# One decoder layer on one core: the sample group's B and C rows sent through DRAM, and three edits around the output projections

## The chip, the cores and the metric

The kernel runs on one core of a Trainium2 chip (trn2). The metric is the device time of one execution in microseconds (us). The median of three runs stands for a kernel.

## The reference, cut to what matters

One layer of a hybrid decoder works on 512 prompt tokens and 8 sample tokens (each with its own past) with the same weights, in float32. A combined projection gives queries and latents for multi-head latent attention (16 heads), and z, x, B, C and dt for a state-space branch (32 heads in 8 groups, state size 128). The part that the change touches first is the state-space step of the 8 sample tokens. For every group, head channel `p`, sample `b` and state index `n`:

```python
state_new[b, p, n] = exp(dt*a) * state[b, p, n] + (dt*x)[b, p] * B[b, n]
y[b, p]            = sum_n C[b, n] * state_new[b, p, n] + d_skip * x[b, p]
...
o_ssm  = rmsnorm_per_group(y * silu(z))
o_attn = attention(...)                                  # for samples: softmax over 2048 paged keys
merged = sigmoid(gate_a) * (o_attn @ w_br_attn) + sigmoid(gate_b) * (o_ssm @ w_br_ssm)
x      = x + rmsnorm(merged @ w_out)
x      = x + rmsnorm(w_down @ relu(w_up @ rmsnorm(x))**2)
```

B and C lie with `n` on the partitions, while the states have `p` on the partitions. So the 128 numbers of B for each sample are needed as a row, the same on all 128 partitions.

## The kernel before, in words

Everything is laid out with channels on the partitions and the T = 520 tokens along the free axis. Each float32 product is made of three passes of TensorE: rounded weight times rounded input, rounded weight times the rest of the input, rest of the weight times rounded input. Weights stream in chunks of 512 KB, in one fixed order, through two slots: SP loads a chunk into `w_stage`, ACT rounds it into `w_hi` (`round_chunk`, L939), POOL subtracts to get `w_lo` (`split_chunk`, L469, four pieces). `linear` (L521) multiplies one chunk of 8 tiles: 48 matmuls of 260 columns, 32 with `w_hi` and then 16 with `w_lo`. Its result goes to one of two slots of the PSUM tensor `lin`; the slots alternate in the order of the lists `..._LIN`, and `free_slot` waits until DVE has released the result before the last (semaphore `lin_free`, counted in DVE's order).

The program's stages are: a start (latents, scan sums), group 0 to 8, eight rows of sample attention, the two output projections, and the MLP (multi-layer perceptron).

*Groups.* Group i projects the inputs of state-space group i (x0, x1, b, c, z0, z1, queries, keys) and, between these projections, does the rest of group g = i - 1: prompt attention (two heads in 8 blocks u), the scan in four pieces c, and the 8 products s0 to s7 with `w_br_ssm`, added to `acc` by DVE (L1729). The last group (i = 8) has gate projections ga0 to ga6 in place of new inputs. For each c, PE issues `scan_front(c)`, `scores(2c+1)`, `project(c+1)` with `transposes(2c)` inside, `values(2c)`, `transposes(2c+1)` (L676), `scan_back(c)`, `scores(2c+2)`, `values(2c+1)`. DVE follows with `normalise` (L1589), `row_max`, `scan_front`, `raw_samples` (L1461, which frees the slot of x0, x1 and so on), `scan_back` (L1616).

*The samples' state in group g.* PE spreads B over the partitions with 8 matmuls of a broadcast column against the identity (`on_all("bB", 2)`, L728), behind s7 and ahead of the first scores and `project(0)`. Each matmul shows as two in the profile. DVE multiplies it from PSUM with dtx (L1643, L1644), adds it to the scaled states (L1647), and then runs `raw_samples(0)`. Behind `project(1)` PE spreads C in the same way (`on_all("bC", 3)`); `sample_y(t)` on DVE multiplies it with the states (L1659) and sums (L1662), for t = 0 in front of `scan_back(0)` and for t = 1 behind `row_max(2)`. The slot of bC is released in `sample_y(1)` (L1661).

*ACT at the end of a group* has `round_chunk(SB)`, the last tanh, 16 scalings of the states (L1044), `round_chunk` of the next group's x0, and at the start of the next group the load of the convolution's history (`history`, L994), `round_chunk` of x1, and then the copies of `project(0)` out of PSUM (L1017, L1018).

*Rows.* Row b scores one sample against its 2048 keys (L796, L804, L809), then PE runs the merge of row b - 1 (`row_merge`, L843 to L847), a gate projection (gb0 to gb7, with two small products inside) and `row_values(b)` (L835). Row 4 has two projections, ga7 and gb4. In SP's queue each row has 4 page loads of keys for row b + 2 (L398), the next weight chunks (L365), and 16 page loads of latent rows; ACT's queue has the other 12 loads of keys (L983).

*Behind row 7* there are: the last merge, `row_out` and the split of the latents on DVE and ACT, then 48 small matmuls of 16 columns with the value weights (L876, here called OV), two copies (L1264, L1809), the branch projection (8 tiles E0 to E7; DVE merges each with the gates, L1819 to L1824) and the output projection (8 tiles F0 to F7). E0 waits for `ov_ready`; F0 waits until all eight merged tiles are there (`mg_ready`).

## Time and profile before

| | |
|---|---|
| median of 3 runs | 1499.13 us (1494.08 to 1499.55) |
| the profiled execution's own time | 1498.6 us |
| its span, first to last instruction | 1496.8 us |
| mean granted TensorE clock | 0.965 |
| PE busy | 1403.4 us, 94% |
| DVE, POOL, ACT busy | 58%, 41%, 38% |
| PE line L521 in the chain that ended last | 52% of the span |
| page loads in the rows stage | DMA engines busy 0.8 to 1.0 of the time |

The span is what the sums below are made in; 1.8 us of the execution's own time lie around it. "Busy" of PE counts overlapping matmuls, so the time of a stretch is read from the start of one instruction to the start of another. The granted clock 1.00 is 2.4 GHz, 0.50 is 1.2 GHz.

### The profile page before, as it was taken

How to read it: one execution, taken by the hardware profiler on the slowest of the kernel's cores; microseconds unless marked ns; L12 is line 12 of the kernel's file. 1: busy time of each engine (PE TensorE's matmuls, PEld its weight loads, DVE VectorE, ACT ScalarE, POOL GpSimd, SP SyncE). 2: the span in 40 equal slices, each digit the busy share in tenths (PEclk: the TensorE clock that was granted, in tenths of full speed). 3: DMA queues.
4: the chain of work that ended last, by engine and by line, in shares of the span. 5: the costliest groups of instructions: out<-in, count | busy, mean ns of one | idle time of the engine just before them, and what ended most of it. 6: DMA issues, size and time to landing. Idle time of an engine off the chain costs nothing.

```text
span 1496.8 us, 28722 instructions
## 1 busy us (share of the span) xinstructions
PE 1403.4 (94%) x11570; PEld 1306.8 (87%) x11570; DVE 860.8 (58%) x1713; ACT 567.9 (38%) x1162; POOL 608.0 (41%) x753
## 2 busy tenths in 40 slices
PE   4999999999999999999999999899579999999994
PEld 4998898988989889898989777799569999999994
DVE  6487878878788787878875443233442222222226
ACT  3344544544444444454544212222233222323221
POOL 4452352443525343352523222344344445444541
PEclk9999999999999999999999999799779999999997
DMA  4223222323233233222245899242113233323231
GB/s 159 85 80 90 80 90 72 103 75 91 75 98 93 71 91 101 77 87 90 74 124 158 264 339 337 77 142 86 42 43 98 87 98 89 97 89 94 87 99 58
DMA packets 109589, 160.47 MB, mean 107 GB/s; under 512 B 16497, under 2 KB 83569, under 8 KB 109457
## 3 DMA queue, kind: packets, MB, share of 16 engines
q1 hardware_dynamic: 54864, 127.32, 27.1%
q10 hardware_dynamic: 54592, 31.33, 7.2%
q8 instruction: 91, 1.49, 0.4%
q14 instruction: 42, 0.34, 0.1%
HBM read 145.87 MB, written 12.74 MB: 106 GB/s over the span
## 4 chain that ended last, share of the span: by engine, by line
PE 66%; DVE 15%; SPq 4%; ACT 4%; issue 2%; DMA 1%; POOL 1%; DVEq 0%; POOLq 0%; ACTq 0%
PE lin L521 52%; SPq L398 3%; PE lin L728 2%; PE Pb L683 1%; PE Pb L554 1%; PE lin L624 1%; DVE arena L1496 1%; DVE arena L1659 1%; DVE ysum L1662 1%; ACT arena L1144 1%; PE Pb L667 1%; DVE sm L1581 1%; PE Pb L676 1%; DMA w_stage<-in_wall 1%; DVE arena L1589 1%
## 5 line engine op out<-in xcount | busy, mean ns | idle before, releaser
L469 POOL TENSOR_TENSOR w_lo<-w_stage,w_hi 128x256 fp32r<-128x256 f32 x736 | 587.2, 829 | 831.1 <-ACT w_hi L939 831.1
L521 PE MATMUL lin<-act_hi,w_hi 128*128 128x260 f32 x1760 | 369.3, 292 | 16.7 <-DVEq L1661 4.3
L521 PE MATMUL lin<-act_lo,w_hi 128*128 128x260 f32 x1760 | 359.2, 286 | 0.0
L521 PEld LDWEIGHTS lin<-act_hi,w_hi 128*128 128x128 f32 x1760 | 276.2, 193 | 32.2 <-issue 21.3
L521 PEld LDWEIGHTS lin<-act_lo,w_hi 128*128 128x128 f32 x1760 | 277.3, 193 | 0.0
L939 ACT ACTIVATE w_hi<-w_stage 128x1024 fp32r<-128x1024 f32 x184 | 193.5, 1052 | 204.5 <-PE lin L521 152.8
L521 PE MATMUL lin<-act_hi,w_lo 128*128 128x260 f32 x1760 | 235.6, 287 | 0.0
L521 PEld LDWEIGHTS lin<-act_hi,w_lo 128*128 128x128 f32 x1760 | 221.7, 191 | 0.4 <-issue 0.4
L521 PE MATMUL lin<-mid_hi,w_hi 128*128 128x260 f32 x1024 | 210.3, 287 | 2.0 <-issue 2.0
L521 PE MATMUL lin<-mid_lo,w_hi 128*128 128x260 f32 x1024 | 207.4, 284 | 0.0
L521 PEld LDWEIGHTS lin<-mid_hi,w_hi 128*128 128x128 f32 x1024 | 160.5, 191 | 3.6 <-issue 3.2
L521 PEld LDWEIGHTS lin<-mid_lo,w_hi 128*128 128x128 f32 x1024 | 159.5, 191 | 0.0
L521 PE MATMUL lin<-mid_hi,w_lo 128*128 128x260 f32 x1024 | 148.8, 282 | 0.0
L521 PEld LDWEIGHTS lin<-mid_hi,w_lo 128*128 128x128 f32 x1024 | 133.7, 188 | 0.0
L1876 DVE TENSOR_TENSOR acc<-acc,lin 128x520 f32<-128x520 f32 x64 | 44.6, 696 | 121.4 <-PE lin L521 120.5
L1855 DVE TENSOR_TENSOR arena<-lin,arena 128x520 f32<-128x520 f32 x32 | 22.4, 699 | 128.9 <-ACT arena L1288 128.9
L1496 DVE SCALAR_TENSOR_TENSOR arena<-arena,small 128x544 f32<-128x544 f32 x64 | 67.4, 1053 | 2.0
L1111 ACT ACTIVATE arena<-Pb,sm 128x128 f32<-128x128 f32 (+1 forms) x64 | 33.8, 528 | 90.8 <-DVE sm L1582 90.8
L1729 DVE TENSOR_TENSOR acc<-acc,lin 128x520 f32<-128x520 f32 x64 | 44.4, 693 | 26.5 <-PE lin L521 25.7
L554 PE MATMUL Pb<-ones,arena 128*65 128x1 f32 x400 | 29.1, 207 | 31.7 <-POOL arena L490 15.5
L554 PEld LDWEIGHTS Pb<-ones,arena 128*65 128x65 f32 x400 | 28.5, 156 | 33.7 <-POOL arena L490 16.3
L1288 ACT ACTIVATE arena<-lin 128x520 f32<-128x520 f32 x32 | 19.4, 606 | 99.6 <-PE lin L521 99.6
(259 smaller groups left out, 1868.3 us busy)
## 6 DMA issues: line engine op xcount, KB each, us to landing
w_stage<-in_wall SPq DMA_DIRECT2D x184, 512.0 KB, 3.6
arena<-in_cache ACTq DMA_DIRECT2D x80, 144.0 KB, 4.3
arena<-in_state ACTq DMA_DIRECT2D x16, 512.0 KB, 5.5
out_stateT<-arena ACTq DMA_DIRECT2D x16, 512.0 KB, 4.1
o_attn<-in_cache SPq DMA_DIRECT2D x64, 128.0 KB, 3.8
arena<-in_cache SPq DMA_DIRECT2D x64, 128.0 KB, 4.2
arena<-in_cache SPq DMA_DIRECT2D x48, 144.0 KB, 3.9
arena<-in_xT SPq DMA_DIRECT2D x8, 520.0 KB, 5.4
```

The lines of the kernel that those rows point to most:

```text
L398: sp.dma_start(dst(j), d["cache"][bass.ds(page, 1), :, lo:hi].rearrange("a p c -> p (a c)")).then_inc(landed, 16)
L469: low = pool.tensor_tensor(w_lo[:, slot, part], w_stage[:, slot, part], w_hi[:, slot, part].bitcast(F32), ALU.subtract)
L521: mm = pe.matmul(lin[:, pl.slot, hf, 0:HALF], w[:, ch.slot, off:off + P], r[:, hf * HALF:(hf + 1) * HALF], start=(k == 0 and p == 0), stop ...
L554: mm = pe.matmul(out[:, c:c + 1], src[:, k, TOKT * c:TOKT * (c + 1)], ones[:, 0:1], start=(k == 0), stop=(k == n - 1))
L728: mm = pe.matmul(lin[:, pl.slot, b // 4, (b % 4) * P:(b % 4 + 1) * P], xc[:, k, SAMP0 + 4 * b:SAMP0 + 4 * b + 1].to_broadcast([P, P]), ide ...
L939: act.activation(w_hi[:, ch.slot, :], w_stage[:, ch.slot, :], ACT.Copy).then_inc(S["w_hi_done"], 1)
L1111: act.activation(Pq[:, pb, 0:(q + 1) * P], Pb[:, pb, 0:(q + 1) * P], ACT.Exp, bias=sm[:, 2 + pb:3 + pb], scale=SM_SCALE, accum_out=sm[:, 4 ...
L1288: act.activation(cols(relu[:, j % 2, :]), lin_cols(pl), ACT.Relu).then_inc(S["relu_a"], 1)
L1496: link(dve.scalar_tensor_tensor(a, raw[:, k, t:t + CONVW], tap(t), a, ALU.mult, ALU.add))
L1729: dve.tensor_tensor(cols(acc[:, m, :]), cols(acc[:, m, :]), lin_cols(pl), ALU.add).then_inc(S["lin_free"], 1)
L1855: dve.tensor_tensor(cols(relu[:, j % 2, :]), lin_cols(pl), cols(relu[:, j % 2, :]), ALU.mult).then_inc(S["lin_free"], 1)
L1876: dve.tensor_tensor(cols(acc[:, m, :]), cols(acc[:, m, :]), lin_cols(pl), ALU.add).then_inc(S["lin_free"], 1)
```

## The change

1. *B and C through DRAM.* DVE copies the 8 sample columns of B and of C into a small tile `smp` (`samples_apart`). ACT stores each 4 KB to a DRAM tensor (`samples_out`), waits for it, and loads it back to all 128 partitions, 512 KB each (`samples_in`), into `B_all` and `C_all`. The 16 spreading matmuls are gone and with them their two places in `lin`. DVE now reads B and C from SBUF, with a stride of 8 elements, and makes and adds the product of one half after the other (`sample_states`). In the first group with a scan (g = 0), `sample_states` moves from ahead of `normalise(0)` to behind `raw_samples(1)`.
2. *A gate moved.* ga7 goes from row 4 to behind the last row's merge, in front of OV.
3. *OV and E0.* OV does the passes of a half with `w_hi` before it waits for `w_lo`. E0 is done by halves of the tokens: the first half (260 prompt tokens) no longer waits for the samples' values.
4. *Output projection singly.* F0 waits for each merged tile at its turn; the E and F loops are written out.

```diff
-STEADY_LIN = (["bB", "x0", "sA0", "x1", "bC", "sA1", "b", "sA2", "c", "sA3", "z0", "z1", "uq0", "uq1", "uk", "uv", "ql"]
+STEADY_LIN = (["x0", "sA0", "x1", "sA1", "b", "sA2", "c", "sA3", "z0", "z1", "uq0", "uq1", "uk", "uv", "ql"]
...
-ROW_GATES = [["gb0"], ["gb1"], ["gb2"], ["gb3"], ["ga7", "gb4"], ["gb5"], ["gb6"], ["gb7"]]
+ROW_GATES = [["gb0"], ["gb1"], ["gb2"], ["gb3"], ["gb4"], ["gb5"], ["gb6"], ["gb7"]]
...
@@ PE, group @@
-                on_all("bB", 2)
                 if g:
                     first_scores()
                     project(0)
+                pe.wait_ge(S["xc_ready"], g * 4 + 4)
...
                     project(c + 1, between=lambda: transposes(u))
-                    if c == 0:
-                        on_all("bC", 3)
...
@@ PE, behind the rows @@
             row_merge(NB - 1)
+            linear(fixed(LIN_LAST), fixed(CH_LAST), K8, act_rhs())
...
+            for half in range(2):
+                ch = fixed(CH_OV + half)
+                pe.wait_ge(S["w_hi_done"], ch.index + 1)
+                for pr in range(4 * half, 4 * half + 4):
+                    for k in range(2):
+                        values_of(pr, k, ((w_hi, olat_hi), (w_hi, olat_lo)), ch)
+                pe.wait_ge(S["w_split"], ch.index + 1)
+                for pr in range(4 * half, 4 * half + 4):
+                    for k in range(2):
+                        mm = values_of(pr, k, ((w_lo, olat_hi),), ch)
...
             pe.wait_ge(S["oa_ready"], KT)
-            pe.wait_ge(S["ov_ready"], 2)
...
-            pe.wait_ge(S["mg_ready"], KT)
...
+            by_halves(fixed(LIN_E), fixed(CH_E), mid_rhs(0, KT), (S["ov_ready"], 2))
+            for m in range(1, KT):
+                linear(fixed(LIN_E + m), fixed(CH_E + m), K8, mid_rhs(0, KT))
+            for m in range(KT):
+                linear(fixed(LIN_F + m), fixed(CH_F + m), K8, act_rhs(), rhs_ready=None if m else (S["mg_ready"], 0))
...
@@ ACT, group @@
+                def samples_out(t):
+                    act.wait_ge(S["smp_ready"], i * 2 + t + 1)
+                    act.dma_start(o["samples"][i, t], smp[:, t, :]).then_inc(S[f"smp_out{t}"], 16)
+
+                def samples_in(t):
+                    act.wait_ge(S[f"smp_out{t}"], i * 16 + 16)
+                    if t == 0:
+                        act.wait_ge(S["st_new"], i * 2)
+                    else:
+                        act.wait_ge(S["xc_ready"], i * 4 + 4)
+                    act.dma_start((B_all, C_all(i))[t], o["samples"][i, t].rearrange("n b -> (n b)").partition_broadcast(P)
+                                  ).then_inc(S[("b_in", "c_in")[t]], 16)
...
                     scaled_state(0)
                     scaled_state(1)
+                    samples_out(0)
                 round_chunk(c_chunk(i, "SB").next())
+                if has_in:
+                    samples_in(0)
+                    samples_out(1)
+                    samples_in(1)
...
@@ DVE, group @@
+                def samples_apart(t):
+                    dve.wait_ge(S[f"smp_out{t}"], i * 16)
+                    dve.wait_ge(S["xc_ready"], i * 4 + (3 + t if has_rest else 4))
+                    dve.tensor_copy(smp[:, t, :], xc[:, 2 + t, SAMP0:CONVW:4]).then_inc(S["smp_ready"], 1)
...
-                link(dve.tensor_tensor(sT[:, 0], bB, spread(dtx[:, 0, :], STATE), ALU.mult))
-                dve.tensor_tensor(sT[:, 1], bB, spread(dtx[:, 1, :], STATE), ALU.mult).then_inc(S["lin_free"], 1)
...
+                def sample_states():
+                    dve.wait_ge(S["xc_ready"], g * 4 + 4)
+                    dve.wait_ge(S["st_scaled"], g * 2 + 2)
+                    link(dve.tensor_tensor(dtx[:, :, :], sdec_all[:, g, :, 0:8], xc[:, 0:2, SAMP0:CONVW:4], ALU.mult))
+                    dve.wait_ge(S["b_in"], g * 16 + 16)
+                    for t in range(2):
+                        new = sT if g else sT_first
+                        link(dve.tensor_tensor(new, B_all.rearrange("p (n b) -> p b n", b=NB), spread(dtx[:, t, :], STATE),
+                                               ALU.mult))
+                        dve.tensor_tensor(sS[:, t], sS[:, t], new, ALU.add).then_inc(S["st_new"], 1)
+                        dve.wait_ge(S["st_new"], g * 2 + (t + 1))
...
                 def sample_y(t):
+                    dve.wait_ge(S["c_in"], g * 16 + 16)
+                    link(dve.tensor_tensor(sC[:, :, :], C_all(g).rearrange("p (n b) -> p b n", b=NB), sS[:, t], ALU.mult))
...
                     if c == 0:
+                        if g == 0:
+                            sample_states()
                         sample_y(0)
```

In group 0, ACT has `samples_out` and `samples_in` for both t at its end, behind the last tanh and ahead of group 1's `history`. Behind the rows, ACT evacuates ga7 between `round_chunk(CH_OV + 1)` and `round_chunk(CH_E)`.

## Rows read from the trace of the kernel before

**Rows 1.** One group by windows: stretch, PE, PEld, DVE, ACT, POOL, PEclk, DMA share, GB/s.

```profile
477.00:566.00 89.00, 87.28 (x707) 79.45 (x707) 73.28 (x144) 43.55 (x108) 36.76 (x40) 1.00 0.30 88
```

**Rows 2.** PE's waits from 209 to 744 us: total, times, longest.

```profile
PE lin L521 <- DVEq L1661: 3.2, 6, 0.5
```

**Rows 3.** Timeline of PE from 391 to 423 us (start, us).

```profile
392.30 1.95 PE L728 MATMUL lin<-ident,arena 128*128 128x128 f32 x16
...
407.70 1.95 PE L728 MATMUL lin<-ident,arena 128*128 128x128 f32 x16
...
409.94 0.44 PE L676 MATMUL Pb<-ident,arena 128*128 128x128 f32 x2
...
422.50 0.65 PE L676 MATMUL Pb<-ident,arena 128*128 128x128 f32 x4
```

**Rows 4.** The chain that ended last, where `project(1)` starts.

```profile
401.96 3.88 PE lin L521 x32
```

**Rows 5.** Timeline of DVE over the same stretch.

```profile
394.35 1.22 DVE L1643 TENSOR_TENSOR arena<-lin,dtx 128x1024 f32<-128x1024 f32 x1 [0.68 <-PE lin L728]
...
396.87 3.27 DVE L1647 TENSOR_TENSOR arena<-arena 128x1024 f32<-128x1024 f32 x2
401.17 0.17 DVE L1461 COPY arena<-lin 128x8 f32<-128x8 f32 x1 [1.03 <-ACT arena L1018]
...
408.66 0.17 DVE L1461 COPY arena<-lin 128x8 f32<-128x8 f32 x1 [1.50 <-ACT arena L1018]
...
412.41 0.60 DVE L1616 SCALAR_TENSOR_TENSOR arena<-arena,small,Pb 128x128 f32<-128x128 f32 x2
...
421.82 0.49 DVE L1589 TENSOR_SCALAR arena<-arena,sm 128x512 f32<-128x512 f32 x1
```

**Rows 6.** Timeline of ACT at the end of the group.

```profile
389.22 1.05 ACT L939 ACTIVATE w_hi<-w_stage 128x1024 fp32r<-128x1024 f32 x1
```

**Rows 7.** DMA issues: count, KB each, median us from issue to landing.

```profile
w_stage<-in_wall SPq DMA_DIRECT2D x184, 512.0 KB, 3.6
...
arena<-in_state ACTq DMA_DIRECT2D x16, 512.0 KB, 5.5
...
arena<-in_hist ACTq DMA_DIRECT2D x8, 64.0 KB, 2.3
```

**Rows 8.** Two lines of DVE by source: ns min/median/max.

```profile
L1647 DVE TENSOR_TENSOR arena<-arena x16: 1224/1590/1642, 132.3 to 753.3; 128x1024 f32<-128x1024 f32 x16
...
L1643 DVE TENSOR_TENSOR arena<-lin,dtx x8: 1223/1224/1224, 129.8 to 749.5; 128x1024 f32<-128x1024 f32 x8
```

**Rows 9.** Timeline of DVE at the start of group 1.

```profile
128.88 0.17 DVE L1461 COPY arena<-lin 128x8 f32<-128x8 f32 x1 [2.13 <-DMA arena<-in_hist]
```

**Rows 10.** Timeline of PE: the first product of rows 4, 5 and 6.

```profile
886.20 0.28 PE L796 MATMUL lin<-qlb,snb 128*1 128x32 f32 x4
...
911.08 0.28 PE L796 MATMUL lin<-qlb,snb 128*1 128x32 f32 x4
...
924.58 0.28 PE L796 MATMUL lin<-qlb,snb 128*1 128x32 f32 x4
```

**Rows 11.** Waits from 840 to 960 us.

```profile
PE lin L521 <- ACT w_hi L939: 1.6, 1, 1.6
```

**Rows 12.** Timeline of PE behind row 7, and at F0.

```profile
956.19 0.35 PE L876 MATMUL lin<-olat_hi,w_hi 128*128 128x16 f32 x1 [2.35 <-issue]
...
967.43 0.77 PE L521 MATMUL lin<-mid_hi,w_hi 128*128 128x260 f32 x2 [0.86 <-issue]
...
1018.27 0.51 PE L521 MATMUL lin<-act_hi,w_hi 128*128 128x260 f32 x2 [2.92 <-DVE act_lo L1824]
```

**Rows 13.** Windows (columns as in rows 1) of three stretches.

```profile
954.00:971.00 17.00, 13.95 (x64) 13.92 (x65) 1.91 (x9) 4.02 (x6) 7.34 (x11) 0.50 0.27 88
189.00:192.00 3.00, 3.00 (x17) 3.00 (x16) 2.62 (x12) 1.24 (x2) 0.80 (x2) 0.56 0.36 115
1019.00:1022.00 3.00, 3.00 (x16) 3.00 (x16) 2.97 (x1) 0.81 (x1) 2.11 (x4) 0.50 0.00 0
```

More of the change, by code:

```diff
@@ L235, in build_layer @@
         sm = sb("sm", [P, 8])
+        smp = sb("smp", [P, 2, NB])
         sms = sb("sms", [P, 8])
@@ L880, in _, with values_of @@
-            mm.then_inc(S["lin_done"], 1)
-            pe.wait_ge(S["oa_ready"], KT)
-            pe.wait_ge(S["ov_ready"], 2)
-            for i in range(0, KT // 2):
-                for j in range(2):
-                    linear(looped(LIN_E, 2, i, j), looped(CH_E, 2, i, j), K8, mid_rhs(0, KT))
-            pe.wait_ge(S["mg_ready"], KT)
-            for i in range(0, KT // 2):
-                for j in range(2):
-                    linear(looped(LIN_F, 2, i, j), looped(CH_F, 2, i, j), K8, act_rhs())
+            def values_of(pr, k, passes, ch):
+                off = (pr % 4) * 256 + k * P
+                for w, x in passes:
+                    r = x[:, k * P:(k + 1) * P].rearrange("p (b h) -> p b h", b=NB)[:, :, 2 * pr:2 * pr + 2]
+                    mm = pe.matmul(lin[:, pl.slot, 0, 16 * pr:16 * pr + 16], w[:, ch.slot, off:off + P], r,
+                                   start=(pr == 0 and k == 0 and w is w_hi and x is olat_hi),
+                                   stop=(pr == 7 and k == 1 and w is w_lo))
+                    if pr % 4 == 0 and k == 0 and w is w_hi and x is olat_hi:
+                        open_chunk(ch, mm)
+                return mm
@@ new lines, in _, with by_halves @@
+            mm.then_inc(S["lin_done"], 1)
+            def by_halves(pl, ch, rhs, second_ready):
+                pe.wait_ge(S["w_hi_done"], ch.index + 1)
+                free_slot(pl)
+                for hf in range(2):
+                    if hf:
+                        pe.wait_ge(second_ready[0], second_ready[1])
+                    part = slice(hf * HALF, (hf + 1) * HALF)
+                    for k in range(KT):
+                        for n in range(2):
+                            mm = pe.matmul(lin[:, pl.slot, hf, 0:HALF], w_hi[:, ch.slot, K8[k]:K8[k] + P], rhs[k][n][:, part],
+                                           start=(k == 0 and n == 0), stop=False)
+                            if hf == 0 and k == 0 and n == 0:
+                                open_chunk(ch, mm)
+                    if hf == 0:
+                        pe.wait_ge(S["w_split"], ch.index + 1)
+                    for k in range(KT):
+                        mm = pe.matmul(lin[:, pl.slot, hf, 0:HALF], w_lo[:, ch.slot, K8[k]:K8[k] + P], rhs[k][0][:, part],
+                                       start=False, stop=(k == KT - 1))
+                mm.then_inc(S["lin_done"], 1)
@@ L1105, in group @@
                     act.wait_ge(S["rows_ready"], 1)
+                    for t in range(2):
+                        samples_out(t)
+                    for t in range(2):
+                        samples_in(t)
                     return
@@ L1674, in group @@
                     if c == 0:
+                        if g == 0:
+                            sample_states()
                         sample_y(0)
@@ L2062, in build @@
     o = {n: nc.dram_tensor("out_" + n, tuple(shape), F32, kind="ExternalOutput").ap() for n, shape in OUTS.items()}
+    o["samples"] = nc.dram_tensor("samples", (GROUPS, 2, P, NB), F32, kind="Internal").ap()
     build_layer(nc, d, o)
```

72 lines of the change are left out of this document (25 added, 47 removed).

## The prediction, on record before the changed kernel ran

> **What bounds the kernel now.** First the windows of one group [rows 1]: of 89.0 us PE is busy 87.28, DVE 73.28, ACT 43.55, and the DMA engines are at 0.30. The reader is to see that PE sets the pace over the whole stage, and that DVE has only some 16 us to spare. Then PE's waits [rows 2]: the one that the change touches by name, for the slot of the spread C, comes six times in six groups and costs 0.5 each. So a group is nearly one long row of matmuls, and what is taken from PE is won, unless another engine cannot follow. Whether it can is read from the timelines of PE, DVE and ACT where the work is taken out [rows 3 to 6]. Behind the groups I read the rows stage [rows 10, 11] and the places around the projections where PE stands still or runs at 1.2 GHz [rows 12, 13].
>
> A note on size first: a measurement of this kernel tells some 0.5% (7.5 us) from no change. The sums are made against the profiled execution's span of 1496.8 us, whose own time is 1498.6, 0.5 below the median of 1499.13.
>
> **B in a steady group.** PE's block for B starts at 392.30 and that for C at 407.70; the latter ends where the next work starts, and transposes(1) follow at 409.94 [rows 3]. A block of 16 instructions starts every 0.12 us, so it costs 1.95; both in eight groups are 31 us of PE's time. That is the most that this part can give, with 0.5 a group for the wait on the slot. Not all of it comes back, because DVE has a chain beside it.
>
> Before, DVE starts the first product at 394.35, when PE has spread B, adds from 396.87 to 400.13, waits for the end of project(0), and frees x0's slot at 401.34 [rows 5]. project(1), which needs that slot, starts at 401.96 [rows 4]. Without B's block PE would be there at 400.0. When is DVE there? ACT begins to round x0's chunk at 389.22, behind the scalings of the states [rows 6]. The store of B now goes out at that place. Its 4 KB are not in the trace; the smallest load there, 64 KB, lands in 2.3 us [rows 7], which gives 391.5. The broadcast load is then issued; it carries 512 KB as a weight chunk does, and that lands in 3.6, the state loads of the same size in 5.5 [rows 7]. I take 3.6, since ACT has just these one or two transfers in flight there and each partition gets one run of 4 KB as in a weight chunk: B is there at 395.1 (397.0 by the other row). DVE then has four operations of 1024 elements. The products from PSUM took 1.22 each, always; the sums with both inputs in SBUF took 1.59 in the median and 1.22 at best, beside POOL's splitting [rows 8]. Now all four read two SBUF tensors. One is over before POOL can start on x1's chunk, which ACT rounds behind these transfers; so 1.22 + 3 x 1.6 + 0.2 of semaphores = 6.2, and x0 is free at 395.1 + 6.2 + 0.2 = 401.5. project(1) starts at 401.5 in place of 401.96. Of B's 1.95 us only 0.45 are left; bounds are 1.95 (B in time, nothing collides) and a loss of 1.4 (5.5 for the landing).
>
> The Trainium skill ("SBUF — State Buffer", section "Who interferes with whom") says that a DVE instruction with two SBUF inputs contends with a GpSimd instruction that reads SBUF, and one with at most one SBUF input does not; rows 8 agree, with 1224 ns at most for one and 1642 for the other. By the rule all four could be slow, which would make 6.6 of the 6.2 and take the rest of the gain.
>
> **C in a steady group.** Before, project(1) ends at 407.70; DVE copies x1's samples at 408.66, and reaches scan_back(0) at 412.41, 4.7 behind the projection [rows 3, 5], because sample_y(0) waited for C's block. Now C has landed long before (its load is issued about 3 us behind B's). The path is 0.96 for the copy, 0.17, then 1.22 to 1.6 for the product, 1.22 and 0.23 for the rest: 3.8 to 4.2. So 0.5 to 0.9 is won on DVE, I take 0.5. From there to normalise(3), which ends at 422.31 [rows 5], DVE hardly stands still, and PE's transposes(3) at 422.50 follow on it [rows 3]: PE loses what it is early. So C's 1.95 us and the 0.53 wait behind it turn into a wait for DVE at transposes(3), all but 0.5. The two copies into smp (0.17 each, as the copy of 8 columns in rows 5) lie in the s phase, where DVE waits for PE.
>
> Sum for a steady group: 0.45 + 0.5 = 0.95 us earlier. It holds for groups 2 to 8 (gates in place of x in the last, same order): 7 x 0.95 = 6.7. Bounds a group: 3.0 (PE at 400.0, 1.95, and 1.0 for C and its wait) and -0.8 (late landing).
>
> **The first group with a scan.** ACT issues the history's load behind both round trips now. In the trace DVE waited 2.13 us for that load already [rows 9]. The store and the return wait hold it back by about 3.4 us (2.3 of landing and two issues), so x0's samples come at 132.3. That alone is covered, for sample_states (5.0) no longer stands ahead of normalise(0). But sample_states now stands ahead of sample_y(0) and scan_back(0), on DVE's full path of the last paragraph. Both together: 3.5 us later than before (between 1 and 5).
>
> **ga7's move.** Row 4 takes 911.08 - 886.20 = 24.9 us, row 5 takes 13.5 [rows 10]. Without ga7 row 4 loses 48 matmuls of 0.12 = 5.8 and the wait of 1.6 for the second chunk [rows 11]: 7.5. The chunks of the later rows have the same place in SP's queue, behind the same page loads; SP issues row 6's and row 7's chunk while PE is a row away. So 7.5 is taken; nothing if the page loads pace the rows.
>
> **Behind row 7.** Before, the last merge ends at 953.84, PE stands for 2.35, OV runs from 956.19 and E0 from 967.43, OV at 1.2 GHz throughout and E0's first 3.6 us too (0.50 up to 971) [rows 12, 13]. By that E0 takes 5.8 + 1.8 = 7.6, to 975.0: 21.1 from the merge. Now: ga7 5.8 with row_out hidden behind it, OV at 2.4 GHz 5.3 (half of 10.4), E0 5.8, whose first half covers the two copies: 16.9. But the clock fell even beside a busy PE, to 0.56 for 189 to 192, behind 32 matmuls of one column at 186 [rows 13], and OV's 48 with 16 columns did not raise it in 11 us. I take it that OV loses the clock halfway (2.7 us, with E0's start): 19.6, 1.5 us less than before. Bounds: 4.2 and 0.
>
> **F0.** PE waits 2.92 for the last merged tile and then runs 3.2 us at 1.2 GHz (the window shows three of them) [rows 12, 13]. The first seven tiles' 28 matmuls with w_hi take 3.4, more than the 2.9 that tile 7 needs. The wait is gone, and the clock's fall with it (1.6): 4.5. Its chunk was split by then already. Bounds 2.9 and 4.5.
>
> **Sum.** -6.7 + 3.5 - 7.5 - 1.5 - 4.5 = -16.7: 1498.6 - 16.7 = 1482.
>
> **The rivals.** *PE gets it all back* (B in time, DVE's chain shorter than I read it): 7 x 3.0 in place of 6.7, 1467 to 1468. For it: DVE has 16 us to spare in a group. Against it: none of them lies between 401 and 422. *The rows are paced by their loads:* page loads need bandwidth and SP's time, and ga7 only covered them: 7.5 less, 1489. For it speaks that the DMA engines are full up to row 6; against it that row 5 takes no more than PE's own 13.5. *B lands like the states,* in 5.5: 0.8 lost a group, 7 x 1.75 more than the forecast: 1494, no change. *The other side:* 128 partitions read the same 4 KB of DRAM, and no row shows such a load. PE waits for it in project(1). Each us beyond 3.6 costs 7 in all; from a landing of 7.1 us the kernel is slower by over 0.5% (1506), at 10 us it is at 1527. No kind of transfer of this size has a median above 5.5 [rows 7]. *The change doesn't do what it says* can't be for B and C; for E0's half it may be, if w_lo is what it waits for, which is in the bounds.
>
> **How the numbers follow.** The forecast (1482, own range 1475 to 1489) has 0.50, all gained back 0.20, rows paced by loads 0.12, landing of 5.5 0.11, slow broadcast 0.07. Range: 1466 (the first rival) to 1495 (the third). Faster by over 0.5% (below 1491.6): 0.49 + 0.20 + 0.09 + 0.02 = 0.80; slower 0.07; the rest 0.13.
>
> **What would show it.** DVE's first product in a group should start about 2.8 us behind the end of s7 and release project(1); PE should wait at project(1) for x0's slot (1.5) and at transposes(3) for normalise, some 3 us a group in all. A group's period should be near 88 us in place of 89. In the first group PE should wait over 3 us. Row 4 should take about 17 us. PE should not stand still between the last merge and E0, the clock fall within OV, and F0 start right behind E7. The prediction is wrong if DVE's waits for b_in are missing or over 4 us, or if rows 5 to 7 grow beyond 13.5.

## The result, and the profile after

| | before | after |
|---|---|---|
| median | 1499.29 us (4 runs) | 1514.39 us (4 runs, 1513.10 to 1517.46) |
| ratio to before, 95% interval | | 1.0112 [1.0085, 1.0139] |
| span of the profiled execution | 1496.8 us | 1511.3 us |
| mean granted clock | 0.965 | 0.960 |

The change makes the kernel slower by 15 us; I had forecast 1482. Of all executions below, two of the kernel e11 took 1719.88 and 7485.51 us, where its other four took 1487.82 to 1493.64, and are left out of its figures. To find the place, I cut the span at one instruction that every group has once: the first matmul of its statistics on PE. "Group" is here the stretch from one such start to the next.

| us | before | after | difference | forecast |
|---|---|---|---|---|
| up to the first statistics | 186.1 | 196.1 | +10.0 | +3.5 |
| six groups behind it, each | 89.06 | 91.64 | +2.58 (15.5 in all) | -0.95 (-5.7) |
| the last group | 88.8 | 93.5 | +4.7 | -0.95 |
| from there to the end | 687.5 | 671.8 | -15.7 | -13.5 |

The tail did about what was said of it, as a sum. The whole miss, 33 us, lies in the part with B and C.

The six groups are not alike. Two of them run at a granted clock of 1.00 throughout and take 90.1 and 90.2 us; the other four have stretches at the lower clock and take 91.0 to 93.4. In the kernel before, the three groups at 1.00 take 88.7 each. So at full clock a group costs 1.4 to 1.5 more, and the rest of the +2.58 is a matter of the clock. Two of the groups, columns as in [rows 1]:

```profile
377.32:470.67 93.35, 86.54 (x671) 78.60 (x671) 77.67 (x145) 42.83 (x107) 39.71 (x40) 0.96 0.31 94
470.67:560.78 90.11, 83.78 (x671) 75.63 (x671) 77.40 (x145) 42.84 (x107) 40.16 (x40) 1.00 0.34 98
```

First PE in the groups: the windows of one group's length and of the whole stretch, and PE's waits over that stretch (total, times, longest), to be held against [rows 1, 2].

```profile
477.00:566.00 89.00, 82.76 (x655) 74.82 (x656) 76.36 (x142) 41.54 (x105) 39.53 (x40) 0.99 0.33 95
209.00:744.00 535.00, 497.60 (x3905) 450.13 (x3905) 451.69 (x836) 248.69 (x622) 232.22 (x232) 0.98 0.33 95
```

```profile
PE Pb L686 <- DVE arena L1647: 17.1, 18, 1.7
PE lin L531 <- DVE arena L1510: 11.6, 6, 2.4
PE Pb L693 <- ACT arena L1165: 6.5, 6, 1.1
```

PE now stands still for DVE at the two places that the prediction named, x0's slot (L1510) and transposes (L1647), and for longer than was forecast. The third wait, for ACT (L1165), is new too. Why DVE is late is read in the timeline of one group, DVE first. It is the longest of the six (93.35). The end of s7 is at 405.1.

```profile
405.92 0.52 DVE L1699 TENSOR_TENSOR dtx<-sdec_all,arena 128x16 f32<-128x16 f32 x1
407.55 2.21 DVE L1703 TENSOR_TENSOR arena<-sga_mid,dtx 128x1024 f32<-128x1024 f32 x1 [1.11 <-DMA sga_mid<-samples]
409.80 1.23 DVE L1705 TENSOR_TENSOR arena<-arena 128x1024 f32<-128x1024 f32 x1
411.06 2.37 DVE L1703 TENSOR_TENSOR arena<-sga_mid,dtx 128x1024 f32<-128x1024 f32 x1
413.46 1.59 DVE L1705 TENSOR_TENSOR arena<-arena 128x1024 f32<-128x1024 f32 x1
415.09 0.17 DVE L1510 COPY arena<-lin 128x8 f32<-128x8 f32 x1
...
423.90 2.45 DVE L1715 TENSOR_TENSOR arena<-arena 128x1024 f32<-128x1024 f32 x1
...
429.42 2.23 DVE L1715 TENSOR_TENSOR arena<-arena 128x1024 f32<-128x1024 f32 x1
```

The transfer is in time: DVE waits 1.11 us for it and starts 2.45 behind the end of s7. But the two products with B (L1703) take 2.21 and 2.37 and the two with C (L1715) 2.45 and 2.23, where they took 1.22 before (B's in [rows 8], C's in the first line here). The lines by source (ns min/median/max), the first of the kernel before and the others of the changed one, show that no product escaped:

```profile
L1659 DVE TENSOR_TENSOR arena<-lin,arena x16: 1214/1220/1225, 141.5 to 769.8; 128x1024 f32<-128x1024 f32 x16
...
L1703 DVE TENSOR_TENSOR arena<-sga_mid,dtx x14: 2111/2244/2430, 225.4 to 778.8; 128x1024 f32<-128x1024 f32 x14
...
L1715 DVE TENSOR_TENSOR arena<-arena x16: 1984/2226/2512, 149.5 to 799.2; 128x1024 f32<-128x1024 f32 x16
```

PE's side of the same group, against [rows 3, 4]:

```profile
415.41 0.48 PE L531 MATMUL lin<-act_hi,w_hi 128*128 128x260 f32 x2 [2.42 <-DVE arena L1510]
...
422.95 0.43 PE L693 MATMUL Pb<-arena 128*64 128x128 f32 x2
...
433.84 0.52 PE L686 MATMUL Pb<-ident,arena 128*128 128x128 f32 x3 [1.66 <-DVE arena L1647]
...
437.37 0.87 PE L693 MATMUL Pb<-arena 128*64 128x128 f32 x6 [1.10 <-ACT arena L1165]
438.64 0.66 PE L686 MATMUL Pb<-ident,arena 128*128 128x128 f32 x4 [0.41 <-DVE arena L1647]
```

project(1) starts 10.3 behind the end of s7, in place of 9.5 (the timeline of PE before has its first matmul at 401.80), and then lasts 7.5 us (415.41 to 422.95) where it took 5.9 before: behind the wait of 2.42 the granted clock falls to the lower level, 0.62 on average from 416 to 420. So here a late DVE is paid twice. That is so in two of the six groups (waits of 2.42 and 2.38); in the other four the wait at project(1) is 1.51 to 1.85 and the clock stays at 1.00 behind it. transposes(3) come 33.5 behind s7, in place of 30.2. The wait for ACT at 437.37 has the same origin: ACT copies the transposed weights only behind the exponentials of the scan (435.67 to 436.94), and these follow DVE's scan_front, which starts at 434.40. It costs 1.1 in every group, and the kernel before doesn't have it.

The DMA issues, against [rows 7], show one cost more. The 4 KB store and both broadcast loads land as expected or nearly; the history's load, which now stands behind a broadcast load in ACT's queue, takes 4.7 in place of 2.3.

```profile
sga_mid<-samples ACTq DMA_DIRECT2D x8, 512.0 KB, 3.6
arena<-samples ACTq DMA_DIRECT2D x8, 512.0 KB, 4.9
arena<-in_hist ACTq DMA_DIRECT2D x8, 64.0 KB, 4.7
...
samples<-smp ACTq DMA_DIRECT2D x16, 4.0 KB, 2.2
```

In the first group with a scan nothing hides these, against [rows 9]. DVE waits 6.80 for the history, so PE waits 6.13; then PE waits 8.87 more for transposes, while DVE does the states and y of the samples (142.3 to 158.1).

```profile
132.32 0.17 DVE L1510 COPY arena<-lin 128x8 f32<-128x8 f32 x1 [6.80 <-DMA arena<-in_hist]
```

```profile
132.63 0.77 PE L531 MATMUL lin<-act_hi,w_hi 128*128 128x260 f32 x2 [6.13 <-DVE arena L1510]
158.74 0.88 PE L686 MATMUL Pb<-ident,arena 128*128 128x128 f32 x3 [8.87 <-DVE arena L1647]
```

The tail: rows 4, 5 and 6 start as follows (against [rows 10]: row 4 takes 14.2 in place of 24.9), and behind row 7 PE goes from the merge (970.98) into ga7 (972.28), OV (979.62), E0 (986.14 and, for its second half, up to E1 at 993.87) and, last line, F0 (against [rows 12]).

```profile
914.58 0.28 PE L793 MATMUL lin<-qlb,snb 128*1 128x32 f32 x4
...
928.80 0.28 PE L793 MATMUL lin<-qlb,snb 128*1 128x32 f32 x4
942.40 0.28 PE L793 MATMUL lin<-qlb,snb 128*1 128x32 f32 x4
...
970.98 0.37 PE L840 MATMUL Pb<-arena,ones 128*128 128x16 f32 x2 [0.64 <-DVE arena L1837]
...
972.28 0.48 PE L531 MATMUL lin<-act_hi,w_hi 128*128 128x260 f32 x2
...
979.62 0.18 PE L871 MATMUL lin<-olat_hi,w_hi 128*128 128x16 f32 x1
...
983.58 0.36 PE L871 MATMUL lin<-olat_hi,w_hi 128*128 128x16 f32 x1
...
986.14 0.57 PE L899 MATMUL lin<-mid_hi,w_hi 128*128 128x260 f32 x1
...
993.87 0.41 PE L531 MATMUL lin<-mid_hi,w_hi 128*128 128x260 f32 x2
...
1034.19 0.40 PE L531 MATMUL lin<-act_hi,w_hi 128*128 128x260 f32 x2
```

PE stands nowhere between the merge and F0 (1034.19). OV runs its small matmuls every 0.11 us up to 983.58 and every 0.21 from there: the clock falls within OV, after 4.0 of its 6.5 us, and is back when E0's second half starts (990.99). F0 starts right behind E7.

### The profile page after: what moved, and what is told of

Its sections match the earlier page's. It is cut to its first block and busy times, and to the rows that moved or that the text cites. A ratio compares the mean times of both kernels' runs of the same rounds, so it can differ in the third digit from the quotient of the medians.

```text
span 1511.3 us, 28274 instructions
## 1 busy us (share of the span) xinstructions
PE 1381.0 (91%) x11314; PEld 1284.0 (85%) x11314; DVE 894.8 (59%) x1729; ACT 565.5 (37%) x1162; POOL 627.5 (42%) x753
## 5 line engine op out<-in xcount | busy, mean ns | idle before, releaser
L479 POOL TENSOR_TENSOR w_lo<-w_stage,w_hi 128x256 fp32r<-128x256 f32 x736 | 606.7, 855 | 825.9 <-ACT w_hi L963 825.9
L531 PE MATMUL lin<-act_hi,w_lo 128*128 128x260 f32 x1760 | 240.5, 291 | 0.0
L531 PEld LDWEIGHTS lin<-act_hi,w_lo 128*128 128x128 f32 x1760 | 226.4, 195 | 0.0
L531 PE MATMUL lin<-mid_hi,w_hi 128*128 128x260 f32 x1008 | 206.9, 287 | 1.1 <-issue 1.1
L531 PE MATMUL lin<-mid_lo,w_hi 128*128 128x260 f32 x1008 | 204.2, 284 | 0.0
L1785 DVE TENSOR_TENSOR acc<-acc,lin 128x520 f32<-128x520 f32 x64 | 44.2, 692 | 22.5 <-PE lin L531 22.3
L564 PE MATMUL Pb<-ones,arena 128*65 128x1 f32 x400 | 27.8, 204 | 31.7 <-POOL arena L500 15.5
L693 PE MATMUL Pb<-arena 128*64 128x128 f32 x320 | 49.3, 286 | 7.6 <-ACT arena L1165 7.6
```

The costliest lines, as they stand in the source:

```text
L479: low = pool.tensor_tensor(w_lo[:, slot, part], w_stage[:, slot, part], w_hi[:, slot, part].bitcast(F32), ALU.subtract)
L531: mm = pe.matmul(lin[:, pl.slot, hf, 0:HALF], w[:, ch.slot, off:off + P], r[:, hf * HALF:(hf + 1) * HALF], start=(k == 0 and p == 0), stop ...
L564: mm = pe.matmul(out[:, c:c + 1], src[:, k, TOKT * c:TOKT * (c + 1)], ones[:, 0:1], start=(k == 0), stop=(k == n - 1))
L693: mm = pe.matmul(Pb[64 * h:64 * h + 64, pb, 0:P], V[:, j, 64 * h:64 * h + 64], PT[:, j * P:(j + 1) * P], start=(j == 0), stop=(j == q))
L1785: dve.tensor_tensor(cols(acc[:, m, :]), cols(acc[:, m, :]), lin_cols(pl), ALU.add).then_inc(S["lin_free"], 1)
```

## The experiments

The theory, from the two traces: DVE reads B and C with a step of 8 elements (32 bytes), and that costs 0.8 to 1.0 us in each of four products a group. Rivals: the transfers themselves, the history's load behind them, and contention with POOL. Every ratio is against the kernel before, run on the same chip beside it.

**e1, the tail parts alone, and e2, the part with B and C alone.** The diff cut in two; of e1 nothing touches the groups, of e2 nothing the tail.

> The kernel before with the moved gate, OV by passes, E0 by halves and F0 tile by tile, and without the transfers through DRAM. The two traces differ by +30.2 us up to the statistics of the last group and by -15.1 us from there to the end. If the two parts act on their own (my theory), this one is 15 us below the kernel before: 1484 us, and groups of 88.7 to 89.3 us. If the tail's gain exists only because the groups reach it in another state of loads and clock (rival), it is less: 1487 to 1495.

> The kernel before with the transfers through DRAM alone, its tail left as it was. Theory: 30 us more than before, 1529 us. Rival (parts depend on one another): well below 1525.

e1: 1483.76 us, 0.9902 [0.9879, 0.9925]. e2: 1527.78 us, 1.0201 [1.0168, 1.0234]. The kernel before had 1496.97 there, so the tail wins 13.2 (forecast 13.5 for it) and B and C through DRAM lose 30.8 (forecast: 3.2 won). The parts add up, 17.6 against 15 measured for both.

**e3, the same transfers, read with a step of 1** (the products take other numbers than B's and C's in their order):

```diff
-  B_all.rearrange("p (n b) -> p b n", b=NB)
+  B_all.rearrange("p (b n) -> p b n", b=NB)
-  C_all(g).rearrange("p (n b) -> p b n", b=NB)
+  C_all(g).rearrange("p (b n) -> p b n", b=NB)
```

> The changed kernel with B_all and C_all read in the order in which they lie (step 1) instead of with a step of 8 elements; it multiplies other numbers than B and C, with the same count of elements. Theory (the step is what the products pay for): the products fall from 2.2 to between 1.22 and 1.6 us, x0's slot comes free some 1.9 us earlier, PE's wait of 2.4 there and the fall of its clock behind it go with it, and scan_back(0) and normalise(3) follow earlier: 4 to 5 us a group, 1475 to 1487 us in all. Rival (two SBUF inputs, and POOL on the same port): the products stay above 2.0 us, 1510 to 1515 us.

1487.57 us, 0.9925 [0.9899, 0.9950]: 27 us less than the changed kernel, from one access pattern. The time is just above my range and far from the rival's. The products by source, and PE's waits over the same stretch as above:

```profile
L1703 DVE TENSOR_TENSOR arena<-sga_mid,dtx x14: 1224/1226/1649, 222.3 to 751.7; 128x1024 f32<-128x1024 f32 x14
```

```profile
PE Pb L686 <- DVE arena L1647: 7.2, 12, 1.0
...
PE lin L531 <- DVE arena L1510: 2.4, 4, 0.8
```

A group behind the first takes 87.98, 3.66 less than in the changed kernel; the four products together (lines of busy time, mean: 2290 and 2299 ns there, 1315 and 1446 here) are 3.66 shorter. That the two figures are equal is in part luck. Two groups here run at 1.00 throughout and take 87.1, 3.0 less than the 90.1 of the changed kernel: of DVE's 3.66 us PE gets 3.0 directly, and the rest of the mean is the clock, which no longer falls behind project(1). PE's wait for ACT (L1165) stays, 6.5 in six groups. The transfers are nearly as before (both broadcast loads 3.8 and 5.0, the history 4.9, the store 1.7), so the rival of the transfers falls.

**e4, the history's load ahead of the last broadcast load** (in group 0 ahead of both), with the step of 8:

```diff
-                if has_in:
-                    history()
...
                 if has_in:
                     samples_in(0)
                     samples_out(1)
+                    if i + 1 < GROUPS:
+                        history(i + 1)
                     samples_in(1)
```

> The changed kernel with the history load issued by ACT ahead of the last broadcast load (in the first group ahead of both). Rival theory (the history's landing of 4.8 us behind a megabyte of broadcast data in ACT's queue costs PE its time): 8 to 14 us less, 1500 to 1506. My theory: only the first group waits for it (6.8 us), and there DVE's chain through sample_states takes part of it back: 2 to 5 us less, 1509 to 1512; steady groups unchanged within 0.3 us each.

1517.39 us, 1.0127 [1.0102, 1.0152], no better than the changed kernel; both my 2 to 5 us less and the rival's 8 to 14 missed. The first statistics come 3.3 earlier (192.88), but a group behind takes 92.8 in place of 91.6: PE's waits at project(1) are 14.3 in place of 11.6, and no group runs at 1.00 throughout. Why is open. The history's place wins something in the first group and nothing in the later ones.

**e5, B and C turned round by the store itself**, 1024 pieces of 4 bytes; the products read with a step of 1 as in e3:

```diff
- act.dma_start(o["samples"][i, t], smp[:, t, :])
+ act.dma_start(o["samples"][i, t].rearrange("b n -> n b"), smp[:, t, :], allow_slow_non_contiguous=True)
- o["samples"][i, t].rearrange("n b -> (n b)")
+ o["samples"][i, t].rearrange("b n -> (b n)")
```

> The changed kernel, but the store to DRAM turns each 128x8 tile of B or C round (1024 pieces of 4 bytes in place of 128 of 32), so that the broadcast load brings B and C with the state index next to itself and all four products read with a step of 1. It computes the whole layer. Theory (the step of 8 costs 0.8 to 1.0 us for each product): products at 1.22 to 1.65 us, total as the run with unit reads, 1485 to 1492, if the store of small pieces lands in up to 3 us (2.2 before). Rival (small pieces are slow): the store lands in over 5 us, B comes 3 or more later, project(1) waits that much in each of seven steady groups, 20 or more in all, and the total is 1508 or more.

1623.16 us, 1.0851 [1.0816, 1.0885]. The products are back at 1224 ns, but the store lands in 11.4 in place of 2.2:

```profile
sga_mid<-samples ACTq DMA_DIRECT2D x8, 512.0 KB, 6.9
...
samples<-smp ACTq DMA_DIRECT2D x16, 4.0 KB, 11.4
```

```profile
362.68 0.77 PE L531 MATMUL lin<-act_hi,w_hi 128*128 128x260 f32 x2 [16.70 <-DVE arena L1510]
```

A group takes 106.5. The rival of this run held: the size of the pieces, not the 4 KB, sets the time. The Trainium skill ("VectorE: DVE Perf Modes", section "The three transpose paths") warns of a transpose made by strides of a plain DMA. The trace agrees: the store takes five times as long to land as the one in its own order.

**e6, C alone with a step of 1** (B in its order with 8, C's product takes other numbers):

```diff
-  C_all(g).rearrange("p (n b) -> p b n", b=NB)
+  C_all(g).rearrange("p (b n) -> p b n", b=NB)
```

> The changed kernel with C alone read with a step of 1 (it so multiplies other numbers in sample_y), B still with 8. Splits the 27 us that unit reads for both gave. If each strided product costs PE the same: 13 us less than the changed kernel, about 1501. If only B's pair counts, since project(1) waits for it, 1514 as the changed kernel; if only C's pair, since transposes(3) waits behind it, 1488.

1499.18 us, 1.0008 [0.9992, 1.0024]. That is 15 of the 27 us for C's pair and 12 for B's. The groups at 1.00 throughout take 88.5 to 88.8, halfway between 90.1 and 87.1: each pair of strided products costs about the same, wherever it stands.

**e7, the step measured by itself**, in the kernel of e1. Behind the layer's last DVE instruction, with POOL and ACT at rest, multiplies and copies of 128x1024 (by source, ns min/median/max). In order: both inputs with step 1; first input with step 2, 4, 8, 16; both inputs with 8; output with 8; copy with 1 and with 8; first input in PSUM with step 1 and 8. The twelfth, not shown, has the first input with step 8 and `dtx` as the second, as in the layer: 1.99. It is one execution (1559.28 us), with four rounds of the twelve within it.

```diff
+ two_b = two.rearrange("p (b n) -> p b n", b=8)
+ out_b = out.rearrange("p (b n) -> p b n", b=8)
+ link(dve.tensor_tensor(out_b, one.rearrange("p (b n) -> p b n", b=8), two_b, ALU.mult))
...
+ link(dve.tensor_tensor(out_b, one.rearrange("p (n b) -> p b n", b=8), two_b, ALU.mult))
...
+ link(dve.tensor_tensor(out_b, psum.rearrange("p (n b) -> p b n", b=8), two_b, ALU.mult))
```

> The kernel with the tail parts alone, and behind DVE's last instruction of the layer twelve more operations on 128x1024 float32 of dead tiles, four times over, with POOL and ACT at rest. Theory (a step in the reading of SBUF costs, whoever else is busy): multiply with steps 1, 2, 4, 8, 16 on the first input goes from 1.22 us up to about 2.0 at 8; the copy of one input with step 8 is also slower than without. Rival (it is two inputs from SBUF, or the broadcast second input, that cost): all steps take the same, 1.6 or more, and the single-input copy is not touched. A step of 8 in PSUM and a step of 8 in the output: not known, 1.2 to 2.2.

```profile
L1941 DVE TENSOR_TENSOR o_attn<-o_attn x4: 1220/1224/1224, 1481.4 to 1538.1; 128x1024 f32<-128x1024 f32 x4
...
L1942 DVE TENSOR_TENSOR o_attn<-o_attn x4: 1224/1224/1225, 1482.6 to 1539.4; 128x1024 f32<-128x1024 f32 x4
...
L1943 DVE TENSOR_TENSOR o_attn<-o_attn x4: 1967/1971/1973, 1483.9 to 1540.6; 128x1024 f32<-128x1024 f32 x4
...
L1944 DVE TENSOR_TENSOR o_attn<-o_attn x4: 1992/1994/1997, 1485.9 to 1542.6; 128x1024 f32<-128x1024 f32 x4
...
L1945 DVE TENSOR_TENSOR o_attn<-o_attn x4: 1876/1877/1886, 1487.9 to 1544.7; 128x1024 f32<-128x1024 f32 x4
...
L1946 DVE TENSOR_TENSOR o_attn<-o_attn x4: 1993/1994/2000, 1489.8 to 1546.6; 128x1024 f32<-128x1024 f32 x4
...
L1947 DVE TENSOR_TENSOR o_attn<-o_attn x4: 2002/2002/2004, 1491.9 to 1548.6; 128x1024 f32<-128x1024 f32 x4
...
L1949 DVE COPY o_attn<-o_attn x4: 694/694/695, 1495.9 to 1552.7; 128x1024 f32<-128x1024 f32 x4
...
L1950 DVE COPY o_attn<-o_attn x4: 1078/1080/1082, 1496.7 to 1553.4; 128x1024 f32<-128x1024 f32 x4
...
L1951 DVE TENSOR_TENSOR o_attn<-lin,o_attn x4: 1224/1224/1225, 1497.8 to 1554.5; 128x1024 f32<-128x1024 f32 x4
...
L1952 DVE TENSOR_TENSOR o_attn<-lin,o_attn x4: 1224/1224/1225, 1499.0 to 1555.8; 128x1024 f32<-128x1024 f32 x4
```

Steps of 1 and 2 are free, from 4 on a multiply takes 1.88 to 1.99 in place of 1.22. A second strided input adds nothing, a strided output costs as much as a strided input, a copy goes from 0.69 to 1.08, and in PSUM a step of 8 is free. With both neighbours at rest the cost is the same, so contention with POOL is not the cause. In the changed kernel's 32 strided products, POOL's part can be read off: 18 of them, in which POOL does not run, take 1.98 to 2.25, and 13, in which it runs throughout, take 2.36 to 2.51 (the remaining one, with POOL in a part of it, 2.41). So a busy POOL goes with some 0.2 more. What keeps the others above 1.99, as at 407.55 (2.21) and 429.42 (2.23) with POOL at rest, is open. The Trainium skill ("Advanced Engine Details and Errata", section "SBUF Cachelines") says that SBUF has lines of 16 bytes and wants at least two hits in one to hide its latency. The run agrees: a step of 2 elements has two hits in 16 bytes, a step of 4 has one.

**e8, the tail parts, and C alone through DRAM**, turned round as in e5; B stays on PE. ACT issues the store behind the scalings and waits for it ahead of the copies of `project(0)`.

```diff
-                    if c == 0:
-                        on_all("bC", 3)
...
@@ ACT, end of a group, and start of the next @@
                     scaled_state(1)
+                    samples_out()
                 round_chunk(c_chunk(i, "SB").next())
...
+                samples_in()
                 raw_evac(0)
```

> The tail parts, and C alone sent through DRAM, turned round in the store and loaded behind the history's load; B stays on PE. It computes the whole layer. Theory (the idea is sound where the transfer has time and the read has a step of 1): C's block of 1.95 us and the 0.5 for its slot go from PE; of these 0.5 to 0.9 a group are kept, 4 to 7 in all, against 1483.8 of the tail parts alone: 1477 to 1480. Rival (DVE's chain up to transposes(3) sets the time, and a product with two SBUF inputs takes up to 1.6 in place of 1.22): no gain, 1483 to 1487.

1531.65 us, 1.0230 [1.0204, 1.0255]. This was my own misplacement: ACT stands for a store that takes 11 us, and the copies behind it free x0's slot late (PE waits 20.6 for L1508 there, in seven waits). My range (1477 to 1480) and the rival's (1483 to 1487) both missed, and it says nothing of the idea.

**e9, B and C turned round on DVE before the store**: each is padded to 32 columns and turned in blocks of 32x32, and the store writes 128 pieces of 128 bytes. The products read with a step of 1.

```diff
-  dve.tensor_copy(smp[:, t, :], xc[:, 2 + t, SAMP0:CONVW:4]).then_inc(S["smp_ready"], 1)
+  link(dve.tensor_copy(smp[:, t, 0:NB], xc[:, 2 + t, SAMP0:CONVW:4]))
+  dve.transpose(smp_t[:, t, :], smp[:, t, :]).then_inc(S["smp_ready"], 1)
...
-  act.dma_start(o["samples"][i, t], smp[:, t, :])
+  act.dma_start(o["samples"][i, t].rearrange("r (q c) -> q r c", q=4), smp_t[:, t, :])
...
-  o["samples"][i, t].rearrange("n b -> (n b)")
+  o["samples"][i, t, 0:NB].rearrange("b n -> (b n)")
```

> The changed kernel with B's and C's 8 columns turned round on DVE before the store (a copy into a tile of 32 columns and a transpose of 32x32 blocks, about 0.2 us more each), stored as 128 pieces of 128 bytes (16 KB), loaded as before as one run of 4 KB to each partition; all products read with a step of 1. It computes the whole layer. Theory (the step cost the 27 us, the small pieces cost what the store turned round in DRAM lost): the store lands in 2.2 to 2.8 us, products take 1.22 to 1.65, total 1485 to 1492 as with unit reads. Rival (something else in the turned layout costs too): above 1500.

1486.89 us, 0.9940 [0.9916, 0.9964], as e3 and within my range, and now with B and C in their right order. The turn costs 0.21 us:

```profile
L1563 DVE STREAM_TRANSPOSE smp_t<-smp x16: 211/211/214, 125.7 to 746.8; 128x32 f32<-128x32 f32 x16
```

**e10, e9 with the history's load first**, the edit of e4 on e9.

> As the one before, and the history's load issued ahead of the last broadcast load. It computes the whole layer. Theory: the first group gets 3 us back, which the later ones keep now that DVE's products are short: 1482 to 1488. Rival (as it was with the step of 8: the later groups give it back): the same as the one before, within 2 us.

1485.02 us, 0.9924 [0.9900, 0.9948]. The first statistics come 3.1 earlier than in e9 (191.8 against 194.9); of it 2 are left in the total, within both intervals.

**e11, e8 repaired**: C alone, turned on DVE, its store behind the rounding of x0's chunk.

```diff
-                    samples_out()
                 round_chunk(c_chunk(i, "SB").next())
+                if has_in:
+                    samples_out()
```

> The tail parts, and C alone through DRAM, turned round on DVE, its store behind the rounding of the next x0 and its load behind the history's; B stays on PE. It computes the whole layer. Theory: with a store that lands in 2.3 us ACT does not stand still, C's 1.95 us and the wait of 0.5 go from PE, of which 0.5 to 0.9 a group are kept: 1477 to 1481 against 1483.8 for the tail parts alone. Rival (transposes(3) waits for DVE all the same, its product with two SBUF inputs taking 1.6 at times): 1482 to 1486.

1490.97 us, 0.9947 [0.9921, 0.9974], not below the tail parts alone (e1, 0.9902). A group takes 89.8, and 89.3 in e1: nothing of C's 1.95 us is kept. Over the same stretch as above PE waits 7.0 for DVE at the transposes and 6.5 for ACT (3.5 and nothing in the kernel before). That is the rival's outcome for a group, but the time lies above the rival's range too (1482 to 1486), since the first group is 3.4 and the last 3.2 longer than in e1.

**e12, e10 with B and C of the first group spread by PE:**

```diff
+                if g == 0:
+                    on_all("bB", 2)
...
+                    if g == 0 and c == 0:
+                        on_all("bC", 3)
```

> As e10 (turned on DVE, history's load first), but in the first group with a scan B and C are spread by PE as in the kernel before, since nothing hides the round trip there. It computes the whole layer. Theory (the first group's 7 us of loss and the steady groups' gain are independent): the first group is over at 185 in place of 192, the later ones are short as in e10, 1477 to 1480. Rival (the later groups lose what the first gains, their pace being set elsewhere): 1483 to 1486, as the tail parts alone and e10.

1481.11 us, 0.9885 [0.9865, 0.9905], between my range and the rival's. The first statistics are back at 185.0 (e10: 191.8) and a group takes 88.6, but the last one takes 94.9.

**e13, e12 with the last group on PE too**, so that six groups use DRAM:

```diff
+                if g == 7:
+                    on_all("bB", 2)
                 if g:
                     first_scores()
...
-                    if g == 0 and c == 0:
+                    if g in (0, 7) and c == 0:
                         on_all("bC", 3)
```

> As e12, but in the last group too B and C are spread by PE, so that only six groups use DRAM. It computes the whole layer. The last group took 88.8 us in the kernel before (from the start of one group's statistics to the next), 93.5 in the changed kernel and 90.7 to 94.9 in the repaired ones. Theory (there PE stands for ga0's slot because ACT waits 12 us for ga1's weight chunk, which shares the DMA engines with both broadcasts; before, B's block on PE filled part of that time): 88 to 89.5 again, 1475 to 1479 in total. Rival (the chunk is late by other loads, the broadcasts have no part in it): the last group stays at 91 or more, 1480 to 1484.

1476.67 us, 0.9868 [0.9847, 0.9888], the fastest here; the groups take 87.4 and the last one 89.0, as the theory had it. (The profiled execution was the fastest of five here and the slowest of six in e12, so the two traces' groups differ by more than the edit: 87.4 and 88.6 for the same six.) In the traces of before, after, e9 and e13 ACT waits 10 to 12 us there for a weight chunk, and in e9, where ga0's slot hangs on it, PE waits 4.08. With B's block on PE it is 0.85 (first line of e9, second of e13):

```profile
759.73 0.49 PE L532 MATMUL lin<-act_hi,w_hi 128*128 128x260 f32 x2 [4.08 <-DVEq L1524]
```

```profile
745.35 0.48 PE L532 MATMUL lin<-act_hi,w_hi 128*128 128x260 f32 x2 [0.85 <-DVEq L1537]
```

Its interval touches that of the tail parts alone (e1, 0.9902 [0.9879, 0.9925]), so of the 5 us between their ratios little is certain. How much of the cost the broadcasts make, and how much the missing block on PE, e13 doesn't part. e11 says a little more: it keeps B's block and has C's broadcast alone, and there ACT waits 13.1 for the chunk and PE 2.80 all the same. So the block alone doesn't hide the delay.

## Why the prediction was wrong

**What bounds the kernel.** Right: PE sets the pace, and what it loses it loses to DVE at project(1) and transposes(3). e3 shows it from the other side: 3.66 us less of DVE make a group at full clock 3.0 shorter. Not foreseen was the third place, the 1.1 us for ACT's copy behind DVE's scan_front; it stays in e3, e9 and e13.

**The step that failed** is in "B in a steady group", the price of the products: "The products from PSUM took 1.22 each, always; the sums with both inputs in SBUF took 1.59 in the median ... so 1.22 + 3 x 1.6 + 0.2 of semaphores = 6.2". I priced the new products by rows of operations with a step of 1, and asked only whether POOL interferes. No row that the prediction shows has a step of 8 in SBUF, so this price was unknown and had to be bounded as such; the list of the change above names the stride. Measured, the four operations take 7.5 (407.55 to 415.05), and project(1) starts 10.3 behind the end of s7 where I had 9.2 (401.5 less 392.3). (The 401.96 that I took for its start before is the chain's row; PE's first matmul is at 401.80, so even the sum's own gain was 0.3 and not 0.45.) The same term fails again in "C in a steady group": "1.22 to 1.6 for the product" was 2.2 to 2.5, twice a group. The products with two SBUF inputs beside GpSimd (POOL), which I did weigh, are the smaller effect: some 0.2 of the 1.0 (see e7). The rule of the Trainium skill that bears on the larger one ("Advanced Engine Details and Errata", section "SBUF Cachelines": at least two hits in a line of 16 bytes) is not in the prediction.

**The transfer** was right, and it was the term that I had doubted most. Store 2.2 (2.3 assumed), broadcast of B 3.6 (3.6), first product 2.45 behind s7 (2.8). The rivals "B lands like the states" and the slow broadcast did not happen. The rival on the other side was slower by a mechanism that isn't there; the real one was none of my rivals. The signs of being wrong that I named (DVE's wait for B missing or over 4 us, rows 5 to 7 longer than 13.5) watched the transfer and the rows; the wait is there (1.11 in the group shown) and row 5 takes 13.6, and neither could show the price of the product.

**A steady group**, forecast -0.95, is right in sign and size once the step is away: -1.1 in e3, -1.4 in e9, and -1.6 for groups at full clock in both (87.1 against 88.7). In the changed kernel the strided products add 3.0 to that, so +1.4 at full clock. The rest of the +2.6 is a cost that I had not counted, the clock: in two of the six groups PE's next projection, behind a wait of 2.4 us, takes 1.6 more at the lower level.

**The first group**, forecast +3.5 (between 1 and 5), came to +10.0. Of this the step is 3.8 (e3: 192.4 against 196.1) and the history behind a broadcast load 3.1 to 3.3 (e4, e10). x0's samples come at 132.32, and I had said 132.3; that is luck, since two errors cancel: the history's load goes out only 1.0 later than before (127.47 against 126.44) where I had 3.4, and its own landing doubles behind the broadcast loads (4.7 in place of 2.3). I called that wait covered. The start of project(1) is (132.63, and 132.39 before), but behind the 6.13 of standing still PE runs it at the lower clock, 0.50 from 132 to 136, and x1's samples come 1.3 later. The rest, some 3 us, goes with the states that now stand ahead of scan_back(0), where they take 7.1 us (142.31 to 149.45). I had 5.0 for them, and no sum that leads from it to the 3.5; e12, which undoes all three, gives everything back.

**The last group** was taken as one of the seven. It differs: a late chunk there leaves ga0's slot taken, which in the kernel before cost PE nothing (ACT waits 10.0 for it, PE no time). Forecast -0.95, measured +4.7, and +2.6 in e9.

**ga7's move**: rows up to the last merge 11.6 shorter (from the last statistics: 131.5 in place of 143.1) where 7.5 were forecast. ga7's own 5.8 and its chunk's wait of 1.6 were right. Of the other 4, 3.3 were in row 4 too (10.7 shorter): before, PE waits 1.64 for the merge of row 3 and then runs at 0.58 of the clock from 892 to 895; now row 4 waits 0.69. The rows are not paced by their loads.

**Behind row 7**: from the merge to E1 22.9 us, before 22.5, so 0.4 lost where 1.5 were to be won. The clock falls within OV as said, but it falls in ga7 too, which I had at full speed: from 1.0 us behind its start a pair of its matmuls takes 0.43 in place of 0.24, for 3.4 us (973.31 to 976.75), and ga7 lasts 7.3 us in place of 5.8.

**F0**: from E1 to the next statistics 88.7 in place of 93.4, 4.7 where 4.5 were forecast.

**The sum** over the tail is 15.7 against 13.5, over the rest +30.2 against -3.2. That the tail's sum is close is in part luck: the rows gave 4.1 more than forecast, and the stretch behind row 7 gave 1.9 less.

## What to carry to other kernels

Price an operand by its access pattern and memory, not by its shape: the page prints 128x1024 for a step of 1 and of 8 alike, and moving a strided read from PSUM to SBUF can cost two thirds more. Where no row has the pattern, keep that cost open and give it a rival of its own. Put the transposition where it is cheap (here 0.21 us on DVE ahead of the store), and look at the first and the last turn of a pipeline apart from the steady ones.

## What the runs showed of the hardware

- DVE, float32, 128x1024, two inputs: 1.22 us for a step of 1 or 2 in SBUF, 1.88 to 2.00 for 4, 8 or 16 on an input or 8 on the output; a copy 0.69 against 1.08; from PSUM 1.22 with a step of 8 too (e7). Beside a busy POOL the same product with a step of 8 takes 2.36 to 2.51. The Trainium skill ("Advanced Engine Details and Errata", section "PSUM Cachelines") speaks of slower matmuls for such patterns in PSUM; for a read by DVE no run here shows a cost.
- 4 KB from DRAM to all 128 partitions, 512 KB in all, land in 3.6 us (median), as fast as a weight chunk that is read once. In e11 and e5 the median is 4.8 and 6.9; why stays open.
- A store of 4 KB lands in 2.2 us as 128 pieces of 32 bytes and in 11.4 as 1024 pieces of 4.
- A load of 64 KB behind a broadcast load in the same queue lands in 4.7 us in place of 2.3.
- PE's granted clock fell to the lower level behind waits of 2.38, 2.42 and 3.58 us at project(1), and stayed at 1.00 behind waits of 1.51, 1.67, 1.75 and 1.85 at the same place (changed kernel, groups 2 to 8).
